# Order and size of the first loads, and three small operations moved from VectorE to GpSimd, in a two-block transformer kernel

## The reference

```
def first_block(x, ...):
    h = rmsnorm(x, norm1_g)
    u = einsum('bsd,de->bse', h, w_in)              # 1024 x 7168
    x_rnn, g_rnn, q, k, v, g_br = split(u)
    xa = causal_dwconv(x_rnn, conv_w, conv_b)       # 4 taps
    ya = rg_lru(xa, w_r, b_r, w_i, b_i, lru_lambda) * gelu(g_rnn)
    yb = moba_attention(rmsnorm(q), rmsnorm(k), v)
    ...                                             # gates, three projections, residual
    ...                                             # second norm, gated FFN of 2816, residual
def reference(x, ...):
    return second_block(first_block(x, ...), ...)   # SWA + MLA attention, FFN of 2816, last norm
```

## Time and profile before

| what | value |
|---|---|
| median of 3 runs | 804.61 us (804.59 to 805.8) |
| the profiled execution | 805.27 us |
| its span, first to last instruction | 803.5 us |
| PE busy in the span | 793.5 us, 99% |
| DVE, ACT, POOL busy | 593.4, 451.5, 85.4 us |
| granted TensorE clock | 1.000 |
| slabs | 133 loads, 139.33 MB read from HBM |

### The profile page before, as it was taken

One profiled execution on the slowest core, in us unless ns is written; L12 is line 12 of the kernel. 1 busy time (PEld: TensorE's weight loads), 2 busy tenths in 40 slices (PEclk: granted clock), 3 DMA queues, 4 the chain that ended last, 5 costly groups with the idle time before them and its releaser, 6 DMA issues.

```text
span 803.5 us, 13337 instructions
## 1 busy us (share of the span) xinstructions
PE 793.5 (99%) x5274; PEld 725.4 (90%) x5274; DVE 593.4 (74%) x713; ACT 451.5 (56%) x593; POOL 85.4 (11%) x94
## 2 busy tenths in 40 slices
PE   8999999999999999999999999999999999999997
PEld 7998889999999899999999899889999888888886
DVE  5994899666567897877877878767787756666664
ACT  6669846556345655444454758747546554444544
POOL 1330231000022100000000432310013000000000
PEclk9999999999999999999999999999999999999999
DMA  8754556434454455455454452442445555554521
GB/s 290 266 168 155 202 175 244 153 113 155 166 201 158 160 210 206 157 201 193 181 196 170 163 195 102 155 160 105 158 157 197 204 185 181 202 180 185 209 104 52
DMA packets 22587, 140.96 MB, mean 175 GB/s; under 512 B 3474, under 2 KB 3730, under 8 KB 6546
## 3 DMA queue, kind: packets, MB, share of 16 engines
q1 hardware_dynamic: 22114, 139.77, 49.0%
q10 hardware_dynamic: 432, 0.62, 0.3%
HBM read 139.33 MB, written 1.05 MB: 175 GB/s over the span
## 4 chain that ended last, share of the span: by engine, by line
PE 96%; DVE 2%; DMA 1%; ACT 0%; SPq 0%; issue 0%
PE pp L1514 20%; PE pp L1477 20%; PE pp L1478 20%; PE pp L1479 20%; PE pp L1516 10%; DMA raw<-in_slabs 1%; PE pp L1628 1%; PE pp L1654 1%; PE pp L1641 1%; PE pp L1617 1%; DVE wlo L908 1%; PE pp L1563 0%; PE pp L1591 0%; PE pp L1575 0%; PE pp L1583 0%
## 5 line engine op out<-in xcount | busy, mean ns | idle before, releaser
L908 DVE TENSOR_TENSOR wlo<-raw,whi 128x2048 fp32r<-128x2048 f32 x129 | 298.4, 2315 | 101.1 <-ACT whi L479 100.9
L479 ACT ACTIVATE whi<-raw 128x2048 fp32r<-128x2048 f32 x129 | 246.3, 1911 | 87.4 <-PE pp L1479 86.5
L1477 PE MATMUL pp<-ahi,whi 128*128 128x256 f32 x768 | 220.6, 287 | 2.8 <-DVE alo L923 2.0
L1514 PE MATMUL pp<-ahilo,whi 128*128 128x512 f32 x704 | 221.4, 396 | 0.0
L1479 PE MATMUL pp<-ahi,wlo 128*128 128x256 f32 x768 | 217.2, 283 | 0.0
L1478 PE MATMUL pp<-alo,whi 128*128 128x256 f32 x768 | 217.2, 283 | 0.0
L1516 PEld LDWEIGHTS pp<-ahilo,wlo 128*128 128x128 f32 x704 | 132.2, 188 | 31.1
L1477 PEld LDWEIGHTS pp<-ahi,whi 128*128 128x128 f32 x768 | 147.1, 191 | 4.5 <-issue 2.8
L1478 PEld LDWEIGHTS pp<-alo,whi 128*128 128x128 f32 x768 | 147.2, 192 | 0.2
L1479 PEld LDWEIGHTS pp<-ahi,wlo 128*128 128x128 f32 x768 | 147.1, 192 | 0.0
L1516 PE MATMUL pp<-ahilo,wlo 128*128 128x256 f32 x704 | 138.3, 278 | 0.0
(11 more groups left out here) (229 smaller groups left out, 824.1 us busy)
## 6 DMA issues: line engine op xcount, KB each, us to landing
raw<-in_slabs SPq DMA_DIRECT2D x125, 1024.0 KB, 4.8
raw<-in_slabs SPq DMA_DIRECT2D x4, 512.0 KB, 9.4
raw<-in_slabs SPq DMA_DIRECT2D x2, 832.0 KB, 4.7
raw<-in_slabs SPq DMA_DIRECT2D x2, 576.0 KB, 4.7
raw<-in_slabs SPq DMA_DIRECT2D x4, 256.0 KB, 6.0
x_res<-in_xT SPq DMA_DIRECT2D x3, 256.0 KB, 6.5
out<-gg SPq DMA_DIRECT2D x3, 256.0 KB, 2.1
gate<-in_final_norm_g SPq DMA_DIRECT2D x1, 512.0 KB, 6.7
```

The source lines that it names most:

```text
L479: e.activation(whi[slot][:, :], raw[slot][:, :], ACT.Copy).then_inc(hi_ready, 1)
L908: e.tensor_tensor(wlo[slot][:, :], raw[slot][:, :], whi[slot][:, :].bitcast(f32), ALU.subtract).then_inc(lo_ready, 1)
L1477: e.matmul(out, lhs[0], rhs[0], start=first, stop=False, skip_group_check=True)
L1514: e.matmul(out[:, m, :], w[m][0], ACT2[:, k, :], start=k == 0, stop=False, skip_group_check=True)
```

## The change

The ACT queue keeps only the parameters. The first piece of x goes to SP, behind the first piece of slab 0, so that pieces of weight and input alternate on one queue. The first half of slab 1 is loaded, rounded and subtracted in two pieces of 512 columns (a quarter of the slab each), and PE waits for the second of them at k = 2. The squares' step 0 comes behind the second of these pieces, steps 1 to 3 behind the second half of slab 1, as before. DVE's operations halfb, qkg and sp[2] go to POOL, ahead of its first fold; DVE waits for them (pool_small) before sp[0].

```diff
+FIRST_PIECES = ((1, 0, 512), (1, 512, 1024), (1, 1024, SLAB), (2, 0, 1024), (2, 1024, SLAB))
...
-        first_in = [sem(f"first_in{i}") for i in range(8)]
+        first_in = [sem(f"first_in{i}") for i in range(4 + len(FIRST_PIECES))]
...
+        pool_small = sem("pool_small")
...
                 e.dma_start(raw[0][:, cols], t["slabs"][0][:, cols]).then_inc(first_in[i], 16)
-                if i:
-                    e.dma_start(X[:, 2 * i:2 * i + 2, :], t["xT"][:, 2 * i:2 * i + 2, :]).then_inc(in_x[i], 16)
-            for i in range(4):
-                s, cols = 1 + i // 2, slice(1024 * (i % 2), 1024 * (i % 2) + 1024)
-                e.dma_start(raw[s][:, cols], t["slabs"][s][:, cols]).then_inc(first_in[4 + i], 16)
+                e.dma_start(X[:, 2 * i:2 * i + 2, :], t["xT"][:, 2 * i:2 * i + 2, :]).then_inc(in_x[i], 16)
+            for i, (s, c0, c1) in enumerate(FIRST_PIECES):
+                e.dma_start(raw[s][:, c0:c1], t["slabs"][s][:, c0:c1]).then_inc(first_in[4 + i], 16)
...
             e.dma_start(par[:, :], t["params"]).then_inc(in_par, 16)
-            e.dma_start(X[:, 0:2, :], t["xT"][:, 0:2, :]).then_inc(in_x[0], 16)
...
-            for i in range(4):
+            for i, (s, c0, c1) in enumerate(FIRST_PIECES):
                 e.wait_ge(first_in[4 + i], 16)
-                hi_part(1 + i // 2, slice(1024 * (i % 2), 1024 * (i % 2) + 1024), i % 2 == 1)
-                if i == 0:
+                hi_part(s, slice(c0, c1), c1 == SLAB)
+                if i == 1:
                     squares(0, 0)
-                if i == 1:
+                if i == 2:
                     for k in range(1, 4):
                         squares(0, k)
...
-                e.wait_ge(*((hi_ready, slot + 1) if done else (first_hi, (0, 3, 4)[slot] + i + 1)))
+                e.wait_ge(*((hi_ready, slot + 1) if done else (first_hi, i + 1)))
...
-            for i in range(2):
-                lo_part(1, slice(1024 * i, 1024 * i + 1024), i, i == 1)
-            for i in range(2):
-                lo_part(2, slice(1024 * i, 1024 * i + 1024), i, i == 1)
-            e.tensor_scalar(halfb[:, :], pcol[:, BR:BR + 16], 0.5, None, ALU.mult)
-            e.tensor_tensor(qkg[:, :], pcol[:, QG:QG + 1], pcol[:, KG:KG + 1], ALU.mult)
-            link(e.tensor_scalar(sp[:, 2, :], pcol[:, LAM:LAM + KD], -1.0, None, ALU.mult))
-            link(e.tensor_tensor(sp[:, 0, :], sp[:, 2, :], pcol[:, LAM:LAM + KD], ALU.max))
+            n = 3
+            for slot, c0, c1 in FIRST_PIECES:
+                lo_part(slot, slice(c0, c1), n, c1 == SLAB)
+                n += c1 < SLAB
+            e.wait_ge(pool_small, 1)
+            e.tensor_tensor(sp[:, 0, :], sp[:, 2, :], pcol[:, LAM:LAM + KD], ALU.max)
             e.tensor_scalar(sp[:, 3, :], sp[:, 2, :], 0.0, None, ALU.max).then_inc(sp_in, 1)
...
+            e.wait_ge(in_par, 16)
+            e.tensor_scalar(halfb[:, :], pcol[:, BR:BR + 16], 0.5, None, ALU.mult)
+            e.tensor_tensor(qkg[:, :], pcol[:, QG:QG + 1], pcol[:, KG:KG + 1], ALU.mult)
+            e.tensor_scalar(sp[:, 2, :], pcol[:, LAM:LAM + KD], -1.0, None, ALU.mult).then_inc(pool_small, 1)
             fold(0)
...
-                        if s in (1, 2) and k % 4 == 0:
-                            e.wait_ge(*((lo_ready, s + 1) if k else (first_lo, s + 3)))
+                        if s in (1, 2):
+                            begun = {(1, 0): 4, (1, 2): 5, (2, 0): 6}.get((s, k))
+                            if begun:
+                                e.wait_ge(first_lo, begun)
+                            if k == 4:
+                                e.wait_ge(lo_ready, s + 1)
```

## The result

| | before | changed |
|---|---|---|
| median | 804.84 us (804.18 to 805.8, 13 runs) | **807.14 us** (804.37 to 808.71, 13 runs) |
| ratio | | 1.0019, 95% interval 1.0011 to 1.0027 |
| profiled execution | 805.27 us | 807.14 us, span 805.3 us |

The changed kernel is slower: the medians lie 2.3 us apart, the ratio makes it 1.5 us, with 0.9 to 2.2 by its interval. The forecast was 804.0 us with a range to 805.3: the result lies outside it and has the other sign. 1.0019 is just under the 0.2% within which the forecast counted a time as the same, but its interval lies clear of 1.

The account below looks back on a forecast made before the run. PE's matmul stream was taken as the bound. Slab 1's quarters won 1.01 us, the fold gave back 0.37, the other parts counted nothing: 0.6 off the 804.61 median gave 804.0 us, range 802.8 to 805.3.

Parts of the forecast that it names:

- What bounds the kernel: Whole kernel: PE is 96% of the chain of waits; nearly all winnable waits lie in the first 16 us.
- what is won by 25 us is carried to the end: PE after the front: no wait until the 0.6 us one in the second block's attention, unless something else becomes late.
- the last piece of x lands at 12.0 still: Slab 0, first piece of x on SP: earlier start only, alo still releases PE at 13.26, worth nothing.
- the bounds: First piece of x on SP: worth between 0 and 1.2 us, the latter if all later pieces come earlier.
- rival B: First loads: transfers get faster on one queue, everything lands 1.0 us earlier, 1.6 us gained, 803.0 us; chance 0.2.
- The quarters: PE before slab 1: first quarter there at about 12.6, the stop vanishes, 1.01 us taken from PE's path.
- the forecast's sum: Path to the squares' sums: 1.01 us won before slab 1, 0.37 given back to the fold, 0.6 taken as gain.
- What is late next: Sums in slab 2: POOL's fold ends at 23.62, PE stops 0.3 to 0.4 us, giving back 0.37.
- this part I cost at nothing: Small operations moved to POOL: DVE's 1.5 us before wlo of slab 3 were off PE's path, so no gain.
- C: Gain lost if the fold ends at 23.9 or later, or DVE's row takes it back: 804.6 us; chance 0.2.
- D: SP's issue order decides: slab 1's second half lands 1.2 us later, fold ends 24.8, 0.5 us slower, 805.1; chance 0.1.

## Why the prediction was wrong

**What bounds the kernel: right for losses, not for gains.** PE's stream is the end, and a stop of 1.80 us at the sums costs 1.77 us. But "what is won by 25 us is carried to the end" failed for the quarters alone: of 0.88 us won behind the sums PE lost 0.43 at ACT's gates at 59.75, where no wait was forecast. In the kernel before PE is already just in time there: the matmul at 60.20 starts 0.21 behind the one ahead of it, where 0.12 is the rule.

**The first piece of x, step failed: "the last piece of x lands at 12.0 still".** The first real matmul came early, as forecast, with no wait at all in the changed kernel (its warm-up ends at 7.5) and at 7.85 instead of 8.49 alone. But the bounds were 0 and a gain. In the kernels with all of x on SP's queue behind the parameters' alone on ACT's, the rate from 2 to 5 us was 164 to 173 GB/s in six profiles, against 216 to 237 in the seven with both queues on x and slab 0. ACT began on the last piece of x at 11.4 in one of the six and at 12.1 to 13.1 in five, and at 11.4 to 12.6 in the seven. The groups overlap there, so one profile proves little; what is clear of noise is the time. Alone the move cost 1.18 us (1.0006 to 1.0024), of which the late x explains 0.7 in the profile. That the rate is the cause is argued from these groups, not tested by itself. I had both rates' nearest row before me and used it for rival B alone, with one sign; a loss from the same row was never worked out.

**The quarters: first step right, the number in part luck.** There was no stop before slab 1 and a stop of 0.17 at the sums. 0.44 us were gained alone where 0.6 were forecast, but not by the forecast's sum: of its 1.01 the fold was to take 0.37 and took some 0.1 (the last piece of x also came 0.3 earlier in that execution, at 11.71), and the gates, which stand nowhere in the sum, took 0.43. Nor is the 0.44 clear of noise; the 1.0 with earlier squares is. That this equals the forecast's 1.01 is chance, since PE still had a stop of 0.64 in slab 0 in its profile, and what moved was DVE's row, by 0.92.

**What is late next: right in place, wrong in size.** The releaser at the sums is POOL. The fold was to end at 23.62; by its start (15.63) and its old durations it would have ended even at 23.0. The term that failed is the 0.74 of its last addition, taken over unchanged from the earlier trace rows: it measured 2.81 and 2.80 in the changed kernel's two profiles and 2.80 in the small operations alone.

**Three operations to POOL, step failed: "this part I cost at nothing".** It costs 1.27 us alone (1.0016, 1.0007 to 1.0025). I asked whether DVE's 1.5 us were on PE's path and what three short operations do to POOL. I didn't ask what moves forward on DVE when they are gone: a subtraction of 2.28 us, to just before POOL's last addition. The forecast's own numbers had the two together: "wlo of slab 3 over by 25.0" puts its start at 22.7 or earlier, and the last addition was to run from 22.88 to 23.62. That the two meeting is the cause is shown from both sides: made to wait for the fold, DVE left POOL its 0.73 and the loss was gone, with the operations still on POOL. The Trainium skill (SBUF — State Buffer, SBUF: two separate sides) has the rule for it, an exclusive lock on the pair of ports that DVE and POOL share, held for a whole instruction. The trace agrees: in the changed kernel wlo ends at 24.49 and the addition 0.58 later, at 25.07, which is most of its own 0.74. I had applied the rule to DVE's first operations near 6 us, where nothing came of it, and not to the end of the fold.

**Half clock: not foreseen.** It takes 1.5 us in the first profile of the changed kernel, as much as any part of the change.

**The sum.** Alone, the queue is +1.18, the small operations +1.27 and the quarters -0.44, together +2.0; measured were +2.3 and +1.96 by the medians, 1.5 and 1.7 by the ratios. That they add up is weaker than it looks: the clock has a share in the changed kernel's median which it hasn't in the parts' profiles, and the early landing in its profile hides what the queue costs in others. The sign of the queue and of the small operations is shown, that of the quarters only together with the earlier squares; the split of the whole to tenths isn't.

**The rivals.** B is refuted: one queue moved less in the first us, not more. C, the gain lost, had the right place, "if it ends at 23.9 or later": the fold ended at 25.07, so its price was set too small. Its other half, that "DVE's row of work up to slab 8 takes the half us back", came true for the quarters alone, at the gates. D had the right sign and an effect through the same queue, but another mechanism and too low a price: the second half of slab 1 was no stop in the changed kernel; what came late, in five of the six profiles with one queue, was x. The Trainium skill (DMA: Bandwidth & Descriptors, Issuing engines are not separate DMA queues), cited for D and B, says that DMAs started by several engines run on the same 16 DMA engines and that starting them on several saves only the sequencer's time. In these runs more is moved with two queues in the first us of the kernel, 216 to 237 GB/s against 164 to 173, at much the same busy share of the DMA engines; the measurement decides here. From 5 to 9 us no gain from two is seen, 278 to 368 GB/s against 346 to 368 with one, with which the page agrees.

**What stays open.** Why the kernels with one queue move less at the start and again from 9 to 13 us: the run with what is wanted last on the second queue fits neither "two queues move more" nor "SP's queue alone decides". And what makes the clock fall: it did behind stops of 2.17 and 2.21 us in the two profiles of the changed kernel, and not behind 1.35 and 1.80 at the same place, nor behind 2.09 at about 14 us with the small operations back, nor behind a longer one, 2.79 at 9.6 us in the run with half of slab 2 on ACT's queue. So the length of a stop alone doesn't decide it.

## What to carry to other kernels

When an operation leaves an engine, look at what moves up in its place and which operation of the other engine it now meets: a short DVE operation between long ones can be the gap in which POOL gets through, and here a wait put back in, with DVE idle, was worth as much as the operations themselves. A row of before gives an operation's duration only for its old neighbours. A gain of PE's lasts only where DVE's and ACT's rows move forward with it: look for the next place at which PE needs them, even if no wait is listed there before. At the start of a kernel, try the first loads over two queues, and put on the second only what is wanted next.

## What was not expected of the hardware

- An addition of 128x256 on POOL took 0.73 to 0.74 us with no DVE subtraction beside it, 1.60 beside wlo of slab 2 and 2.80 to 2.81 when it started 0.05 to 0.06 us behind a DVE subtraction of 2.28 us.
- Behind a stop of 2.2 us of PE the granted clock was 0.52 for 3.5 us (0.56 for 3 us in the second profile), and full behind a stop of 2.8 us at another place. The mean clocks suggest the fall in about half of the changed kernel's runs.
- With one queue for the first loads 164 to 173 GB/s were moved from 2 to 5 us, with two 216 to 237, at much the same busy share of the DMA engines, 0.80 to 0.84 and 0.81 to 0.88. From 9 to 13 us it was 312 to 343 against 370 to 409, in twelve of the thirteen with only SP's loads under way.
